# Gathers, result stores and the router of three mixture-of-experts stages, reordered

## What is computed

```python
def hier_moe(h, w_rg, b_rg, w_re, b_re, w_gate, w_up, w_down):
    g_logits = (h @ w_rg).astype(jnp.float32) + b_rg.astype(jnp.float32)
    p_group = jax.nn.softmax(g_logits, axis=-1)
    p_top, g_idx = lax.top_k(p_group, 1)
    e_logits = ((h @ w_re).astype(jnp.float32) + b_re.astype(jnp.float32)).reshape(
        T, N_EXPERT_GROUPS, EXPERTS_PER_GROUP)
    e_logits = jnp.take_along_axis(e_logits, g_idx[:, :, None], axis=1)[:, 0]
    e_top, e_local = lax.top_k(e_logits, TOP_K_IN_GROUP)
    weights = p_top * jax.nn.softmax(e_top, axis=-1)
    expert_id = g_idx * EXPERTS_PER_GROUP + e_local
...
    def expert_block(args):
        xb, e = args
        return (jax.nn.silu(xb @ w_gate[e]) * (xb @ w_up[e])) @ w_down[e]
...
    contrib = (w_sorted[:, None] * y_disp[dest].astype(jnp.float32))
    out = jnp.zeros((T, D), jnp.float32).at[t_sorted].add(contrib)
```

## Time and profile before

| | |
|---|---|
| median of 3 runs | 3223.39 us (3221.16 to 3237.9) |
| the profiled execution | 3233.42 us |
| its span in the trace | 3231.7 us |
| mean granted TensorE clock | 0.879 of full speed |
| PE busy | 2530.7 us (78%) |
| DVE busy | 1255.3 us (39%) |
| ACT busy | 944.7 us (29%) |
| POOL busy | 364.4 us (11%) |
| read from and written to HBM | 560.18 MB, 35.92 MB |

### The profile page before, as it was taken

One profiled execution on the slowest core, in us unless ns is written; L12 is line 12 of the kernel. 1 busy time (PEld: TensorE's weight loads), 2 busy tenths in 40 slices (PEclk: granted clock), 3 DMA queues, 4 the chain that ended last, 5 costly groups with the idle time before them and its releaser, 6 DMA issues. The chain is left out here.

```text
span 3231.7 us, 51558 instructions
## 1 busy us (share of the span) xinstructions
PE 2530.7 (78%) x17988; PEld 1959.7 (61%) x17989; DVE 1255.3 (39%) x2672; ACT 944.7 (29%) x1720; POOL 364.4 (11%) x706
## 2 busy tenths in 40 slices
PE   4974698589889859699898388894969998658883
PEld 4963688445445438476677266663847677636662
DVE  3447334311111145447443432235734753432224
ACT  2233323112112122236322133332234532213232
POOL 0000000012111110000000233231000000113233
PEclk9987899789999979799999598896979999768887
DMA  3201231489999942122121669944122121289972
GB/s 119 80 1 39 66 117 53 181 354 407 414 409 412 404 153 75 33 66 66 50 57 56 276 234 348 349 182 139 53 57 58 49 63 44 65 347 363 362 298 100
DMA packets 208903, 565.75 MB, mean 175 GB/s; under 512 B 26198, under 2 KB 170198, under 8 KB 184192
## 3 DMA queue, kind: packets, MB, share of 16 engines
q1 hardware_dynamic: 191056, 538.71, 45.1%
q0 software_dynamic: 17712, 25.23, 2.4%
HBM read 560.18 MB, written 35.92 MB: 184 GB/s over the span
## 5 line engine op out<-in xcount | busy, mean ns | idle before, releaser
L997 PE MATMUL ps<-e_wgu,e_xT 128*64 128x128 f32 (+1 forms) x2688 | 426.4, 321 | 41.2 <-issue 22.5
L997 PEld LDWEIGHTS ps<-e_wgu,e_xT 128*64 128x64 f32 x2688 | 344.4, 147 | 165.2 <-issue 116.7
L999 PE MATMUL ps<-e_wgu,e_xT 128*64 128x128 f32 (+1 forms) x2688 | 426.1, 321 | 0.0
L999 PEld LDWEIGHTS ps<-e_wgu,e_xT 128*64 128x64 f32 x2688 | 344.0, 147 | 0.0
L1020 PE MATMUL ps<-e_wd,e_hidT 128*64 128x512 f32 x1112 | 303.8, 682 | 5.4 <-ACT e_hidT L1051 4.0
L1903 PE MATMUL ps<-t_hT,t0a_t0g_w 128*128 128x512 f32 x768 | 199.2, 411 | 4.6 <-DVE t0a_t0g_w L1925 2.4
L1903 PE MATMUL ps<-t_hT,t1a_t1g_w 128*128 128x512 f32 x768 | 198.0, 409 | 4.6 <-DVE t1a_t1g_w L1925 2.4
L1162 DVE COPY e_y_out<-e_y 128x512 f32<-128x512 f32 x108 | 46.3, 429 | 372.9 <-DMA e_dram_y<-e_y_out,e_choicecur 267.4
L447 POOL TENSOR_TENSOR all_x<-all_x,ln_rows 128x1024 f32<-128x1024 f32 x16 | 48.2, 3040 | 1262.5 <-DVE all_x L440 1262.5
L1170 DVE TENSOR_TENSOR e_hid<-e_silu,ps 64x128 f32<-64x128 f32 (+1 forms) x210 | 67.1, 334 | 299.5 <-ACT e_silu L1048 293.0
L1048 ACT ACTIVATE e_silu<-ps 64x128 f32<-64x128 f32 (+1 forms) x210 | 63.9, 304 | 378.5 <-PE ps L999 377.5
(11 more groups left out here) (604 smaller groups left out, 4738.6 us busy)
## 6 DMA issues: line engine op xcount, KB each, us to landing
e_wgu<-in_w_exp_gate_up SPq DMA_DIRECT2D x54, 2048.0 KB, 9.2
e_wgu<-in_w_gate_up SPq DMA_DIRECT2D x22, 4096.0 KB
e_wd<-in_w_down SPq DMA_DIRECT2D x32, 2048.0 KB
e_wd<-in_w_exp_down SPq DMA_DIRECT2D x64, 1024.0 KB
m_both<-in_w_gate_up SPq DMA_DIRECT2D x10, 4096.0 KB, 37.8
r_hT<-in_w_exp_gate_up SPq DMA_DIRECT2D x10, 2048.0 KB
t0a_t0g_raw<-in_w_in SPq DMA_DIRECT2D x32, 512.0 KB
t1a_t1g_raw<-in_w_in SPq DMA_DIRECT2D x32, 512.0 KB
```

Source lines behind the costliest of these rows:

```text
L997: nc.tensor.matmul(ps_gu[q][0:SLOTS], xT[:, c, :], wgu[s][:, 0, c, span], start=c == 0, stop=c == DC - 1)
L999: last = nc.tensor.matmul(ps_gu[q][SLOTS:P], xT[:, c, :], wgu[s][:, 1, c, span], start=c == 0, stop=c == DC - 1)
```

## The change

- `ExpertRing` and `Router` are allocated around norm and `moe`. In the norm stage, SP issues the router's loads and then the loads of all ring slots but the last (`load_first`); in `moe` it stores the rows, waits for the logits and the stored rows, and loads the last slot.
- The router's logits come by token tiles: 4 tiles of 8 matmuls with `hT` as weights and 36 columns. The copy and the turns back are gone. The counts come before the ranks; the number of blocks is rounded from the count in three steps; tables are written after the slots; `tokcol` comes before `choicecol`; the weights of the results come last.
- `landing`, `y`, `tokcur` and `choicecur` have two buffers, used in turn. VectorE copies y from PSUM itself, at the end of its block; ScalarE no longer does, and `y_out` and `move_y` are gone.
- TensorE turns the first half of the hidden product ahead of the next block's rows.
- GpSimd's loop runs over pairs of blocks, with an even number of blocks always; two gathers are issued before it, and 4 spare stores behind them.
- The final adds go token tile by token tile.

```diff
@@ rms_rows @@
                 for dst, src in loads:
                     sp.dma_start(dst, src).then_inc(landed, 16)
+                if ring is not None:
+                    ring.load_first(sp)
@@ post_norm @@
                 sp.dma_start(rows[:, 1], row_b.partition_broadcast(P)).then_inc(bias_landed, 16)
+                if router is not None:
+                    for dst, src in router.loads:
+                        sp.dma_start(dst, src).then_inc(router_landed, 16)
+                    ring.load_first(sp)
+                    sp.wait_ge(router_landed, 16 * len(router.loads))
...
+class ExpertRing:
...
+        self.n = 3 * 512 // ff
...
+    def load_first(self, sp):
+        for s in range(self.n - 1):
+            for m in range(2):
+                self.load(sp, s, s, m)
...
@@ moe, SP @@
                 sp.dma_start(rows_dram.rearrange("(t p) d -> p t d", p=P), h_rows).then_inc(rows_stored, 16)
...
+                sp.wait_ge(logits_ready, 1)
+                sp.wait_ge(rows_stored, 16)
+                for m in range(2):
+                    ring.load(sp, RING - 1, RING - 1, m)
...
@@ moe, TensorE @@
-                pe.wait_ge(router_landed, 64)
-
-                for c in range(DC):
-                    last = nc.tensor.matmul(ps[0:NG + NE, 6, :], router[:, c, :], hT[:, c, :], start=c == 0, stop=c == DC - 1)
-                last.then_inc(logitsT_ready, 1)
-                pe.wait_ge(logitsT_copied, 1)
                 for t in range(TT):
-                    last = nc.tensor.transpose(ps[:, t, 0:NG + NE], logitsT[:, t * P:(t + 1) * P], ident[0:NG + NE, 0:NG + NE])
+                    for c in range(DC):
+                        last = nc.tensor.matmul(ps[:, t, 0:NG + NE], hT[:, c, t * P:(t + 1) * P], router.w[:, c, :],
+                                                start=c == 0, stop=c == DC - 1)
                 last.then_inc(logits_ready, 1)
...
+                for t in range(TT):
+                    last = nc.tensor.matmul(ps[:, 5, 0:NE], k["ones"][:], both[:, t, :], start=t == 0, stop=t == TT - 1)
+                last.then_inc(counts_ready, 1)
...
+                        turn_hid(g, 0)
                         pe.wait_ge(rows_staged, g + 2)
                         turn()
...
+                        turn_hid(g, 1)
...
@@ moe, ScalarE @@
-                        act.wait_ge(y_ready, g + 1)
-                        act.wait_ge(y_moved, g + 1)
-                        nc.scalar.copy(y[:], ps_y).then_inc(y_copied, 1)
                         act.reg_add(done, done, 1)
...
@@ moe, VectorE @@
+                def rounded(out, src, scale, shift, least=0.0):
+
+                    link(vec.tensor_scalar(out[0], src, scale, shift, ALU.mult, ALU.add))
+                    link(vec.tensor_scalar(out[1], out[0], ROUND, None, ALU.add))
+                    link(vec.tensor_scalar(out[2], out[1], -ROUND, least, ALU.add, ALU.max))
+                    return out[2]
+
+                dve.sem_inc(y_copied, 1)
...
+                dve.wait_ge(counts_ready, 1)
+                blocks = rounded([nblk[:, n] for n in range(3)], ps[:, 5, 0:NE], 1.0 / SLOTS, 0.5 - 0.5 / SLOTS, 1.0)
...
                     with dve.Fori(0, blocks_of(dve, e)):
                         g = dve.snap(done)
-                        move_y(g)
...
                         turn_copy(g + 2)
-                        stage_rows(g + 2)
+
+                        dve.wait_ge(rows_gathered[0], (g + 4) // 2 * 16)
+                        dve.wait_ge(rows_gathered[1], (g + 3) // 2 * 16)
+                        vec.tensor_scalar(gathered[:], landing[:, bass.ds(g % 2, 1)].rearrange("p one d -> p (one d)"),
+                                          1.0, None, ALU.mult).then_inc(rows_staged, 1)
+
+                        dve.wait_ge(y_stored[0], (g + 4) // 2 * 16)
+                        dve.wait_ge(y_stored[1], (g + 3) // 2 * 16)
+                        dve.wait_ge(y_ready, g + 1)
+                        vec.tensor_scalar(y[:, bass.ds(g % 2, 1)].rearrange("p one d -> p (one d)"), ps_y,
+                                          1.0, None, ALU.mult).then_inc(y_copied, 1)
...
+                dve.wait_ge(choicecur_ready, dve.snap(done))
+                dve.sem_inc(y_copied, 1)
...
@@ moe, GpSimd @@
+                for n in range(2):
+                    gather(n, n)
+                for n in range(4):
+                    nc.gpsimd.dma_start(spare_dram[n:n + 1], ident[0:1, 0:SLOTS]).then_inc(y_stored[n % 2], 16)
+                pool.wait_ge(choicecol_ready, 1)
+                pool.wait_ge(table_ready, 2)
+                n_pairs = pairs_of_blocks(pool)
+                with pool.Fori(0, n_pairs) as pair:
+                    for p in range(2):
+                        n = pair * 2 + p
+                        pool.wait_ge(rows_staged, n + 1)
+                        gather(n + 2, p)
+                        pool.wait_ge(y_copied, n + 2)
+                        store(n, p)
```

More of the change, by code:

```diff
@@ L789, in moe @@
     y_dram = nc.dram_tensor(f"{name}_dram_y", [4 * S, D // 2], F32).ap()
-    spare_dram = nc.dram_tensor(f"{name}_dram_spare", [2, SLOTS], F32).ap()
+    spare_dram = nc.dram_tensor(f"{name}_dram_spare", [4, SLOTS], F32).ap()
     with Stage(nc, name) as st:
[L793 to L800, removed]
+        y = st.sb("y", [P, 2, D // 2])
+        at_pos = y[:, 0].rearrange("p (j t s) -> p j t s", j=2, t=TT)
+        xT = st.sb("xT", [P, DC, SLOTS])
+        at_blk = xT[:].rearrange("p c s -> p (c s)")[:, 0:2 * TT * TABLE].rearrange("p (j t b) -> p j t b", j=2, t=TT)
+        landing = st.sb("landing", [SLOTS, 2, D])
+        gathered = st.sb("gathered", [SLOTS, D])
+        silu = st.sb("silu", [P, 2, HALF])
+        hid = st.sb("hid", [P, 2, HALF])
+        hidT = st.sb("hidT", [P, NF, SLOTS])
         logits = st.sb("logits", [P, TT, NG + NE])
@@ L980, in turn, with turn_hid @@
                     last.then_inc(turned, 1)
+                def turn_hid(g, q):
+                    pe.wait_ge(hid_ready, g * 2 + (q + 1))
+                    for f in range(HF):
+                        last = nc.tensor.matmul(ps_hid[q][:, f * SLOTS:(f + 1) * SLOTS],
+                                                hid[SLOTS:P, q, f * P:(f + 1) * P], ident[SLOTS:P, SLOTS:P],
+                                                start=True, stop=True)
+                    last.then_inc(hid_turned, 1)
                 pe.wait_ge(rows_staged, 1)
@@ new lines, in _ @@
+                dve.wait_ge(rank_ready, 1)
+                link(vec.tensor_tensor(slot[:], ps[:, 4, 0:TT * NE].rearrange("p (t e) -> p t e", e=NE),
+                                       ends[:, 2:3].to_broadcast([P, TT, NE]), ALU.add))
+                for j in range(2):
+                    link(vec.tensor_tensor(picked[:, j], slot[:], hot[:, j], ALU.mult))
+                link(vec.tensor_reduce(slotf[:], picked[:].rearrange("p j t e -> p (j t) e"), AX_X, ALU.add))
+                in_block = rounded([blk[:, n] for n in range(3)], slotf[:], 1.0 / SLOTS, 0.5 / SLOTS - 0.5)
@@ new lines, in _ @@
+                vec.tensor_tensor(flat, flat, k["choice"][:].rearrange("p j t -> p (j t)").unsqueeze(2).to_broadcast(
+                    [P, 2 * TT, TABLE]), ALU.mult).then_inc(hot_slots_ready, 1)
+                vec.tensor_copy(table[0:1, 0], blocks[0:1]).then_inc(table_ready, 1)
+                vec.tensor_copy(table[0:1, 1], ends[0:1, 0])
+                n_pairs = rounded([pairs[:, n] for n in range(3)], ends[0:1, 0, NE - 1:NE], 0.5, 0.25)
+                vec.tensor_copy(pair_table[:], n_pairs).then_inc(table_ready, 1)
@@ L1091, in _ @@
+                vec.tensor_tensor(choicecol[:], part[:, 2], part[:, 0], ALU.add).then_inc(choicecol_ready, 1)
                 dve.wait_ge(exp_ready, 1)
@@ L1229 @@
+                with pool.Fori(0, n_pairs) as pair:
[5 more added lines that the diff above has]
+                        store(n, p)
+                for n in range(2):
+                    pool.wait_ge(rows_gathered[n], n_pairs * 16 + 16)
 class Columns:
```

313 lines of the change are left out of this document (125 added, 188 removed).

## The result

The changed kernel takes 3323.7 us (median of 4 runs, 3321.8 to 3328.0), the kernel before 3223.7: a ratio of 1.0298, interval 1.0272 to 1.0324. It is 3.0% slower. I had forecast 3330 us, from 3200 to 3450. The profiled executions have spans of 3322.3 and 3231.7 us, 90.6 us apart; the medians are 100 us apart, because the profiled run before lies some 10 us over its median.

A forecast was written before the change was run, and what follows sets the result against it. Bound: full DMA engines in e0, a gather period of 3.0 us plus flight in e2. Loops +141, starts -38, tail +3 give +106 on the profiled 3233.4 us: 3339, as median 3330, range 3200 to 3450.

The forecast's parts named there:

- The bound: Block loops: GpSimd's order makes each gather wait for the previous store and y copy, so gathers overlap only at the start.
- the signs I had named: Expected in the profile: strict store-gather order, store waits gone, longer gather waits, under 300 GB/s in e2, earlier first up projections.
- The fixed part: Block loop's period apart from the gather's flight: copies, issues and waits summing to 6.0 us, against 3.0 before.
- The flight: Time from the end of a gather's issue to its rows' copy: 10.1, 4.0 and 4.4 us in e0, e1, e2.
- rival 2: Block loops: same cycle, but a quiet queue shortens flights below 2.7 (e1), 3.1 (e2), 8.7 us (e0); 3200 us; 14%.
- The mechanism of the flight: Block loops: flight taken between quiet and loaded queue values, the gather being mostly past the gate/up load; 4.4 us in e2.
- Starts: Before each stage's blocks: earlier logits, shorter routing and shorter first flights give -14, -12, -12, together -38 us.
- The router: Logits by token tiles: 64 passes taken as 9.5 us (14.7 at half clock), logits some 5 us earlier.
- Priced at nothing: Second result buffer with y copy on VectorE, hidden product's first half ahead of the turn, loads in the norm: 0 each.
- Tail: After the blocks: same 24 adds, plus a dummy gather and store for e2's odd block count; +3 us.
- Rival 3: Block loops: flights stay at loaded values, as the store goes 2 us ahead of the gather; +300 - 35, 3488 us; 20%.
- Rival 1: Block loops: the buffers make gathers overlap and loops run at the next limit; median 3068 us; 5%.

The follow-up runs named there:

- x1: Changed kernel with rows gathered four row sets ahead instead of two, buffers unchanged; 3098.8 us, ratio to before 0.9609.
- x2: Changed kernel with rows gathered three row sets ahead instead of two, GpSimd's order still store then gather; 3113.8 us, ratio to before 0.9653.
- x3: Changed kernel with VectorE's copy of y put ahead of its copy of the landed rows, still gathering two ahead; 3254.6 us.
- e0: Not a run: the first of the kernel's three mixture-of-experts stages; first to last up projection's start 487.8 us before, 514.2 after the change.
- x9: Kernel before's block loop with the changed kernel's router, loads in the norm and spare stores; 3183.2 us, ratio to before 0.9879.
- x6: Changed kernel whose expert refills bring only 64 KB each of their 1 to 4 MB, all instructions and waits kept; 3048.5 us.
- x7: Changed kernel with SyncE holding each gate/up weight refill until GpSimd has issued the gather that would otherwise follow it; 3247.3 us.
- x4: Changed kernel with four one-element multiplies put on GpSimd between each store and the next gather; 3341.8 us.
- x10: Changed kernel with sixteen one-element multiplies put on GpSimd between each store and the next gather; 3464.7 us.
- x11: Changed kernel, still two ahead, with the y copy waiting for the previous block's store to land, as with one result buffer; 3323.8 us.
- x8: Changed kernel with the first expert loads moved out of the norm into the stage, behind the rows' store; 3327.3 us.

## Why the prediction was right, and where only its sum was

*The bound.* "Gather g+3 stands behind store(g), and store(g) behind the copy of block g's y" is what the rows show and what x1, x2 and x3 each undo in another way. Of the signs I had named, these came: strictly store, gather; store waits gone; 208 and 184 us of gather waits in e1 and e2; 236 and 271 GB/s; the last y copies of e1 7.4 to 8.2 us apart (the very last 6.8). One came in e0 only: the first up projection was to be 12 to 14 us sooner after the stage's start, and was 12.5, 9.9 and 8.5.

*The fixed part*, 6.0, is 5.4: the y copy's end to the store's issue is 1.14, not 1.41, the y copy starts before the rows' copy ends (1.28 together, not 1.38), and the 0.2 for waits is nothing.

*The flight*, 10.1, 4.0 and 4.4, is 10.2, 4.7 and 4.8. So 16.1, 10.0 and 10.4 against 15.5, 10.1 and 10.2: in e1 two errors, 0.7 in the flight and 0.6 in the fixed part, cancel, which is luck, and in e0, where the flight was right, the error of the fixed part stands alone. From first to last block the loops cost +108 where +141 was forecast, +26 for e0's +48 and +33 for e2's +44. Part of that gap may be credit of the starts: in x9 the old loops of e1 and e2 are 8 and 14 us shorter too. By medians the starts alone are worth -40.5 (3223.7 to 3183.2) and the loop on top of them +140.5, against -38 and +141 in the forecast. That these agree so well is partly luck: only 28 of the 40.5 lie in the starts by the rows, and the starts were to give 38. In total +106 was forecast; +90.6 was measured on the profiled runs and +100 by medians.

The Trainium skill's "DMA: Bandwidth & Descriptors" ("Anatomy of one DMA") gives 2.0 us plus the bytes over 436 GB/s, by which an estimate for a gather is 2.6 us. The traces agree in an emptied queue (x6: 2.5 in e1) and not in the real one (4.7 to 10.2). The prediction says that with 2.6 us its sum would be rival 2's, which is not so: rival 2's 3200 has 9.2 us in e0, and 2.6 in all stages gives nothing in e0, -4 in e1, -15 in e2 and -35 elsewhere, some 3170 us.

*The mechanism of the flight* was the weak step. I took it for a number between an empty queue's and a full one's, and took the gather to be mostly past the gate/up load. But that load is issued 1.9 us after the y copy's end in the pair shown, ahead of the gather, whose issue ends 4.1 us after it; it is so in 28 of 69 blocks. So the 4.7 and 4.8 are means of two groups, some 2.5 and 8.0 us, and not a size that any block has. The order of issue matters by itself (x7). In e1 and e2 a long gather lands about when the load ahead of it does (where the trace has both landings, 0.2 us before to 2.1 after), so a later issue is partly forgiven (x4, x10) and an earlier one partly wasted (x3). In e0 that picture does not hold: there gathers landed up to 11 us before the load ahead of them.

*Starts*, by sections: -38 forecast, -31 measured. The router was to give 5 us in each stage. The logits come 5.3, 3.8 and 0.9 us sooner after the norm's start. The 64 passes took 10.9, 12.5 and 13.9 us at the clock the rows show (0.66, 0.56, 0.50; the last is the lower level, 1.2 GHz, all the way):

```profile
609.20:620.10 10.90, 10.78 (x64) 10.67 (x64) 1.81 (x2) 1.28 (x1) 0.00 (x0) 0.66 1.01 434
1819.40:1831.90 12.50, 12.47 (x64) 12.35 (x64) 1.81 (x2) 1.26 (x1) 0.00 (x0) 0.56 0.99 419
2892.50:2906.40 13.90, 13.84 (x64) 13.70 (x64) 1.81 (x2) 1.25 (x1) 0.00 (x0) 0.50 1.01 426
```

I took 9.5, "the clock rising early". My own bound of 14.7 at the lower level was the nearer one for e2. The 5.3 of e0 is no steady gain either: in nine of the twelve other profiled runs with this router, e0's passes took 12.8 to 13.0 us at a clock of 0.53 to 0.55, with the logits only 2.1 us sooner than before, and over e1 and e2 of all thirteen the clock was 0.50 in 21 of 26. From the logits to the first turned rows the gain is 7.3, 6.0 and 7.6, where 9.4 was forecast for e0 and 7.1 for e2: the gather is issued 4.6, 5.6 and 5.6 us sooner (4.1 forecast), and its flight falls from 11.3, 7.0 and 6.4 to 8.6, 5.1 and 3.0 (to 6 in e0 and 3.5 in e2 forecast).

*Priced at nothing*: the second result buffer (x11: 0), the order of turning, and the loads in the norm, where x8 gives +3.6 and x9 hints at a gain that I had missed. *Tail*: +3 forecast, +8 measured; e1 has a share of it (+3.1), since its last y copy now waits for rows beyond the last block; in x3, where it doesn't, e1's tail is 28.0 us, as before. The +5 in sections that the change doesn't touch stays unexplained; x1 and x9 don't show it.

*Rivals.* Rival 2 needed flights under 2.7 and 3.1 us in e1 and e2: x6 has them, with little weights. Rival 3 is refuted, with 4.7 and 4.8 for its 6.0. Rival 1, 3068 us, described no effect of this change, but x1 comes within 31 us of it.

## What to carry to other kernels

Before crediting a second buffer, write down for each transfer which instruction issues it, what that engine does just before, and which step frees what that step waits for; two buffers overlap only if the issue for the next item doesn't depend on the result of this one. Here the number gathered ahead (two or four) decided between 3.0% slower and 3.9% faster with the same buffers. A small transfer with someone waiting is best issued ahead of a large one that nobody needs yet (x7: 76 us). Where the flights of one kind of transfer fall into two groups, look first at what was issued just ahead of each.

## What was not expected of the hardware

In e1 and e2 of the changed kernel the flight of a gather of at most 256 KB is 6.9 to 9.3 us where a 2 MB load was issued 1.3 to 3.5 us before the end of its own issue, and 1.3 to 4.0 where the last such load was 7.4 us back or more; no gather fell between. The DMA engines as a whole were busy only 0.63 and 0.73 of these loops. And a waiting TensorE also computes more slowly: in e1 and e2 the granted clock fell from 0.89 and 0.87 to 0.84, and a matmul of the down projections took 783 ns on average, against 605 in x1 at 0.98 and 0.97 (from the page of the changed kernel, then of x1):

```profile
L1037 PE MATMUL ps<-r_down,e_hidT 128*64 128x512 f32 x568 | 184.4, 783 | 0.0
```

```profile
L1037 PE MATMUL ps<-r_down,e_hidT 128*64 128x512 f32 x568 | 137.5, 605 | 0.0
```
